# Sharing the first modulation between two engines, turning scaled rows, and moving modulation pieces between attentions

## The reference

```python
def adaln_modulation(c, w, b):
    mod = jax.nn.silu(c) @ w + b
    return [m[:, None, :] for m in jnp.split(mod, N_MOD, axis=-1)]
...
    for layer in range(DEPTH):
        shift_m, scale_m, gate_m, shift_f, scale_f, gate_f = adaln_modulation(c, *ada[layer])
        pre_m, post_m, pre_f, post_f = norms[layer]
        h = rmsnorm(x, pre_m) * (1.0 + scale_m) + shift_m
        x = x + gate_m * rmsnorm(mixers[layer](h), post_m)
        h = rmsnorm(x, pre_f) * (1.0 + scale_f) + shift_f
        x = x + gate_f * rmsnorm(swiglu(h, *ffns[layer]), post_f)
    return x
```

## Time and profile before

| | |
|---|---|
| median of three runs | 2046.96 us (2045.36 to 2047.48) |
| the profiled execution | 2044.72 us, span 2042.9 us |
| PE busy | 1922.0 us (94% of the span) |
| DVE busy | 1378.7 us (67%) |
| ACT busy | 986.7 us (48%) |
| POOL busy | 263.4 us (13%) |
| mean granted clock of PE | 0.978 |
| chain that ended last | PE 75%, DVE 14%, ACT 3%, issue 2% |

### The profile page before, as it was taken

One profiled execution on the slowest core, in us unless ns is written; L12 is line 12 of the kernel. 1 busy time (PEld: TensorE's weight loads), 2 busy tenths in 40 slices (PEclk: granted clock), 3 DMA queues, 4 the chain that ended last, 5 costly groups with the idle time before them and its releaser, 6 DMA issues.

```text
span 2042.9 us, 33499 instructions
## 1 busy us (share of the span) xinstructions
PE 1922.0 (94%) x13340; PEld 1773.0 (87%) x13340; DVE 1378.7 (67%) x2511; ACT 986.7 (48%) x1432; POOL 263.4 (13%) x121
## 2 busy tenths in 40 slices
PE   5899899988998789999998999999999999999998
PEld 5887799988967589998997889999998888999997
DVE  4898765647956664335756548988878887666665
ACT  5445544454435354445554545566653334444444
POOL 1001044430001024441000047100000000000000
PEclk8999999999999799999999999999999999999999
DMA  7663466645654245555444344477776866555452
GB/s 300 228 203 127 157 250 247 234 179 199 205 181 169 73 166 195 186 186 181 165 145 142 127 145 166 166 209 220 219 220 227 300 255 227 187 225 196 176 204 106
DMA packets 94234, 392.82 MB, mean 192 GB/s; under 512 B 7648, under 2 KB 41584, under 8 KB 55552
## 3 DMA queue, kind: packets, MB, share of 16 engines
q1 hardware_dynamic: 94080, 390.69, 55.0%
HBM read 372.83 MB, written 15.73 MB: 190 GB/s over the span
## 4 chain that ended last, share of the span: by engine, by line
PE 75%; DVE 14%; ACT 3%; issue 2%; DMA 0%; POOL 0%; DVEq 0%; ACTq 0%
PE ps L563 10%; PE ps L565 10%; PE ps L564 10%; PE acc L559 9%; PE acc L560 9%; PE acc L561 9%; DVE wlo L1281 3%; PE acc L563 3%; PE acc L565 3%; PE acc L564 3%; DVE arena L1310 2%; PE ps L1236 1%; PE acc L1236 1%; PE ps L626 1%; PE ps L1009 1%
## 5 line engine op out<-in xcount | busy, mean ns | idle before, releaser
L2300 ACT ACTIVATE whi<-raw 128x1024 fp32r<-128x1024 f32 x559 | 589.5, 1059 | 494.3 <-PE acc L561 274.1
L1281 DVE TENSOR_TENSOR wlo<-raw,whi 128x1024 fp32r<-128x1024 f32 x460 | 567.9, 1242 | 312.3 <-ACT whi L2300 311.4
L563 PE MATMUL ps<-hhi,whi 128*128 128x256 f32 x1824 | 521.2, 286 | 9.5 <-ACT hhi L2412 5.4
L564 PE MATMUL ps<-hlo,whi 128*128 128x256 f32 x1824 | 516.6, 283 | 0.0
L565 PE MATMUL ps<-hhi,wlo 128*128 128x256 f32 x1824 | 516.6, 283 | 0.0
L563 PEld LDWEIGHTS ps<-hhi,whi 128*128 128x128 f32 x1824 | 350.2, 192 | 14.6 <-ACT hhi L2412 6.1
L564 PEld LDWEIGHTS ps<-hlo,whi 128*128 128x128 f32 x1824 | 350.3, 192 | 2.9
L565 PEld LDWEIGHTS ps<-hhi,wlo 128*128 128x128 f32 x1824 | 350.1, 192 | 0.0
L1281 POOL TENSOR_TENSOR wlo<-raw,whi 128x1024 fp32r<-128x1024 f32 x99 | 245.2, 2480 | 683.1 <-ACT whi L2300 682.8
L559 PE MATMUL acc<-whi,chi 128*128 128x512 f32 x752 | 295.6, 393 | 3.5 <-DVE wlo L1281 1.9
L560 PE MATMUL acc<-whi,clo 128*128 128x512 f32 x752 | 294.0, 391 | 0.0
(11 more groups left out here) (443 smaller groups left out, 2418.6 us busy)
## 6 DMA issues: line engine op xcount, KB each, us to landing
raw<-in_peer_down SPq DMA_DIRECT2D x64, 1024.0 KB, 5.0
raw<-in_peer_up SPq DMA_DIRECT2D x64, 1024.0 KB, 5.1
arena<-in_ada SPq DMA_DIRECT2D x80, 512.0 KB, 4.8
raw<-in_w_gate SPq DMA_DIRECT2D x22, 1024.0 KB, 4.8
raw<-in_w_up SPq DMA_DIRECT2D x22, 1024.0 KB, 5.2
raw<-in_w_down SPq DMA_DIRECT2D x22, 1024.0 KB, 4.8
arena<-spill SPq DMA_DIRECT2D x14, 1024.0 KB, 7.0
spill<-hT_t SPq DMA_DIRECT2D x22, 448.0 KB, 6.4
```

The lines of the kernel that those rows point to most:

```text
L563: e.matmul(out, hi, xh, start=start, stop=False, skip_group_check=True)
L564: e.matmul(out, hi, xl, start=False, stop=False, skip_group_check=True)
L1281: e.tensor_tensor(out=lo, in0=w, in1=hi.bitcast(F32), op=ALU.subtract).then_inc(*X(("lo", j)))
L2300: e.activation(hi, w, ACT.Copy, scale=1.0).then_inc(*self.A(("hi", j)))
```

## The change

It has five parts.

1. The prologue's modulation: each of the four groups is shared. DVE does parts 0, 1, 4 and 5, ACT scales parts 2, 3, 6 and 7 (`BY_PE`), and PE sums those four and then DVE's sum. The first weight slab's transfer goes ahead of the last quarter's; piece 0's goes to just before slab 2. Three correction cuts leave POOL for DVE.
2. Norms: DVE scales the rows of x themselves (`ve_unit`), and PE turns them by transposes; `pe_rows` does transposes as well.
3. At the junctions, one cut of the next stage's first weights on ACT goes ahead between the squares, the one after it goes behind the high parts; DVE's goes behind the second tile (where the norm has shifts).
4. Seven modulation pieces leave the NSA stage (`ada=False`) and are done in GLA: two after w_ngate, three after the second compression, two ahead of the last head (`pe_pieces`, `ve_pieces`).
5. In NSA the normalisation of GLA's output moves ahead of w_nvs, cuts come ahead of the scores, and the turn of the compressed probabilities goes into the first branch.

```diff
-FIRST = (("w_low", 0, 0), ("w_low", 0, 1), ("w_low", 1, 0), ("w_glr", 0, 0), ("w_mqk", 0, 0))
+FIRST = (("w_glr", 0, 0), ("w_mqk", 0, 0))
+BY_PE = (2, 3, 6, 7)
...
     def pe_norm(...)
...
-            e.wait_ge(*self.at("diag", nm, tt))
             for j in range(8):
+                if j % 4 == 0:
+                    e.wait_ge(*self.at("unit", nm, tt, j // 4))
                 o = (j % 2) * 256 + tt * 128
-                i = e.matmul(self.banks.tile(nm, "turned", j // 2)[:, o:o + 128], x[:, tt, j * 128:(j + 1) * 128],
-                             m.diag[:, tt, :], start=True, stop=True, skip_group_check=True)
+                i = e.transpose(self.banks.tile(nm, "turned", j // 2)[:, o:o + 128], m.upd[:, tt, j * 128:(j + 1) * 128],
+                                m.ident)
...
     def pe_rows(...)
...
-                i = e.matmul(ps[:, j * 128:(j + 1) * 128], bc(col[:, 4 * half + j:4 * half + j + 1], [128, 128]), self.m.ident,
-                             start=True, stop=True, skip_group_check=True)
+                i = e.transpose(ps[:, j * 128:(j + 1) * 128], bc(col[:, 4 * half + j:4 * half + j + 1], [128, 128]),
+                                self.m.ident)
...
+    def pe_pieces(self, e, n):
+        for _ in range(n):
+            self.pe_ada(e)
...
     def pe_pro(...)
...
+            for k in BY_PE:
+                e.wait_ge(*self.at("scaled", g, k))
                 for j in range(4):
+                    e.matmul(ps[:, j * 128:(j + 1) * 128], m.ada4[:, g, k // 2, (k % 2) * 512 + j * 128:
+                                                                 (k % 2) * 512 + j * 128 + 128], m.ones,
+                             start=k == BY_PE[0] and j == 0, stop=False, skip_group_check=True)
+            e.wait_ge(*self.at("summed", g))
+            for j in range(4):
+                i = e.matmul(ps[:, j * 128:(j + 1) * 128], m.acc4[:, g, j * 128:(j + 1) * 128], m.ones, start=False,
+                             stop=True, skip_group_check=True)
...
     def pe_gla(...)
...
         t.then_inc(*self.P(("full", "w_ngate"), ("whole", "w_ngate", 0), ("gated", "P")))
+        self.pe_pieces(e, 2)
...
         self.pe_cmp_hidden(e, 1)
+        self.pe_pieces(e, 3)
         self.pe_cmp_turn(e, 1)
         e.wait_ge(*self.at("out", "gla_state", 2, 2))
         for h in range(4):
+            if h == 3:
+                self.pe_pieces(e, 2)
...
     def pe_nsa(...)
...
-        self.pe_linear(e, "w_nks", 0, 8, 2, m.hH, m.hL)
-        self.pe_linear_tok(e, "w_nvs", 0, 8, m.hH, m.hL)
+        self.pe_linear(e, "w_nks", 0, 8, 2, m.hH, m.hL, ada=False)
+        self.pe_linear_tok(e, "w_nvs", 0, 8, m.hH, m.hL, ada=False)
...
-                self.pe_out(e, "w_out1a", range(at, at + 2), m.cH, m.cL, at == 0, False, "mix1_post", "gla")
+                self.pe_out(e, "w_out1a", range(at, at + 2), m.cH, m.cL, at == 0, False, "mix1_post", "gla", ada=False)
...
-    def ve_diag(self, e, nm, tt):
+    def ve_unit(self, e, nm, tt, x):
         m = self.m
         e.wait_ge(*self.at("root", nm, tt))
-        e.tensor_scalar(out=m.diag[:, tt, :], in0=m.ident, scalar1=m.small[:, 50 + tt:51 + tt], scalar2=None,
-                        op0=ALU.mult).then_inc(*self.V(("diag", nm, tt)))
+        for half in range(2):
+            sl = slice(512 * half, 512 * half + 512)
+            e.tensor_scalar(out=m.upd[:, tt, sl], in0=x[:, tt, sl], scalar1=m.small[:, 50 + tt:51 + tt], scalar2=None,
+                            op0=ALU.mult).then_inc(*self.V(("unit", nm, tt, half)))
...
     def ve_gla(...)
...
         self.ve_windows(e, 0)
+        self.ve_pieces(e, 2)
...
         self.ve_windows(e, 1)
+        self.ve_pieces(e, 3)
         self.ve_cmp_turn(e, 1)
+        self.ve_pieces(e, 2)
...
     def se_junction(...)
...
         self.se_acc_square(e, post, 1, 0)
+        self.cut_hi(e, self.W.last(first, 0) + 1)
         self.se_x_square(e, norm, post, 0, 0)
...
     def se_normed(...)
...
-        if first:
-            self.cut_hi(e, self.W.last(first, 0) + 2)
         for jj in range(4):
...
+        if first:
+            self.cut_hi(e, self.W.last(first, 0) + 2)
...
     def sync(...)
...
         for g in range(4):
             for h in range(2):
+                if (g, h) == (3, 1):
+                    e.dma_start(self.W.slab(0)[0], D["w_low"][0]).then_inc(self.W.slots[0], 16)
...
-        self.sp_ada(e, 0)
...
+            if n == 0:
+                continue
+            if n == 2:
+                self.sp_ada(e, 0)
```

More of the change, by code:

```diff
@@ L736, in pe_pro @@
         m = self.m
-        self.pe_norm(e, "mix0", m.x)
+        self.pe_norm(e, "mix0")
         for g in range(4):
             ps = self.banks.take(e, "mod", g)
[L740 to L748, removed]
-                for j in range(4):
-                    i = e.matmul(ps[:, j * 128:(j + 1) * 128], m.acc4[:, g, j * 128:(j + 1) * 128], m.ones, start=j == 0,
-                                 stop=True, skip_group_check=True)
+            for k in BY_PE:
+                e.wait_ge(*self.at("scaled", g, k))
+                for j in range(4):
+                    e.matmul(ps[:, j * 128:(j + 1) * 128], m.ada4[:, g, k // 2, (k % 2) * 512 + j * 128:
[5 more added lines that the diff above has]
+                             stop=True, skip_group_check=True)
             i.then_inc(*self.P(("full", "mod", g)))
@@ L922, in pe_mix1 @@
         self.P.mark("end", "ffn0", "P")
-        self.pe_norm(e, "mix1", m.x)
+        self.pe_norm(e, "mix1")
         self.banks.order = ALL
@@ L1084, in pe_mix2 @@
         self.P.mark("end", "ffn1", "P")
-        self.pe_norm(e, "mix2", m.x)
+        self.pe_norm(e, "mix2")
         self.banks.order = ALL
@@ L1178, in pe_route @@
         m = self.m
-        self.pe_norm(e, "peer", m.x)
+        self.pe_norm(e, "peer")
         self.banks.order = ALL
@@ L1311, in ve_ada, with ve_pieces @@
                                            op1=ALU.add).then_inc(*V(*([("ada", s)] if k else [])))
+    def ve_pieces(self, e, n):
+        for _ in range(n):
+            self.ve_ada(e)
     def ve_ada_until(self, e, layer, part):
@@ L1384, in ve_normed @@
         whole(1)
+        if first:
+            self.cut_lo(e, V, self.W.last(first, 0) + 1)
         low(0)
@@ L1453, in ve_sum @@
         self.ve_eps(e, norm, 0, 48)
-        self.ve_diag(e, norm, 0)
+        self.ve_unit(e, norm, 0, self.m.x)
         self.ve_add_x(e, post, 1, 1)
@@ L1874, in ve_nsa @@
                     *V(*([("hvx",)] if ht and j == 3 else [])))
-        self.ve_linear(e, "w_nks", 0, 8, 2)
-        self.ve_linear_tok(e, "w_nvs", 0, 8)
-        e.wait_ge(*self.at("full", "vb"))
-        e.tensor_tensor(out=m.vb, in0=bc(self.banks.tile("vb")[:, 0:64].unsqueeze(1), [128, 8, 64]),
-                        in1=bc(m.kc("ind").unsqueeze(2), [128, 8, 64]), op=ALU.mult).then_inc(*V(("out", "vb")))
+        self.ve_linear(e, "w_nks", 0, 8, 2, ada=False)
         e.wait_ge(*self.at("rstd", "gla"))
@@ L1888, in ve_nsa @@
                 *V(("normed", "gla", j)))
+        self.ve_linear_tok(e, "w_nvs", 0, 8, ada=False)
+        e.wait_ge(*self.at("full", "vb"))
+        e.tensor_tensor(out=m.vb, in0=bc(self.banks.tile("vb")[:, 0:64].unsqueeze(1), [128, 8, 64]),
+                        in1=bc(m.kc("ind").unsqueeze(2), [128, 8, 64]), op=ALU.mult).then_inc(*V(("out", "vb")))
         for eng in "PA":
@@ L1925, in ve_nsa @@
                 self.ve_scores(e, f"nsa{qt}{br}", 8, nk, 0.125, lambda hs, n: m.ab[:, qt, hs, 0:nk], m.St1,
-                               gate=m.ng[:, qt, 8 + 8 * br:16 + 8 * br])
-                self.ve_out(e, "w_out1a", range(at, at + 2))
+                               gate=m.ng[:, qt, 8 + 8 * br:16 + 8 * br],
+                               ahead=self.W.last("w_out1a", 2 * at + 1, 512) + 2)
+                self.ve_out_by_rows(e, "w_out1a", range(at, at + 2), ada=False)
                 self.ve_turn(e, f"nsa{qt}{br}", 8, nk, m.PT1[br])
-            e.wait_ge(*self.at("full", "pct", qt))
-            e.tensor_copy(m.pct, self.banks.tile("pct", qt)[:, 0:128]).then_inc(*V(("out", "pct", qt)))
+                if br == 0:
+                    e.wait_ge(*self.at("full", "pct", qt))
+                    e.tensor_copy(m.pct, self.banks.tile("pct", qt)[:, 0:128]).then_inc(*V(("out", "pct", qt)))
             self.ve_bank_split(e, f"nsa{qt}", m.hH, m.hL, qt)
@@ L2378, in se_junction, with se_norm @@
         self.se_root(e, norm, 1, 48)
-    def se_norm(self, e, nm, src, at=48, ahead=None):
+    def se_norm(self, e, nm, src, at=48, ahead=None, first=None):
         for tt in range(2):
             for half in range(2):
+                if tt and half and first:
+                    self.cut_hi(e, self.W.last(first, 0) + 1)
                 self.se_x_square(e, nm, src, tt, half, at)
@@ L2694, in se_nsa @@
                 at = 4 * qt + 2 * br
+                self.cut_hi(e, self.W.last("w_out1a", 2 * at + 1, 512) + 2)
                 self.se_scores(e, f"nsa{qt}{br}", 8, nk, m.St1)
```

(2 more changed lines are left out.)

105 lines of the change are left out of this document (60 added, 45 removed).

## The result

The changed kernel takes 2032.26 us (median of four runs, 2030.82 to 2034.59) against 2046.16 for the kernel before (four runs). The ratio is 0.9931, with a 95% interval of 0.9916 to 0.9947: faster by 14 us, between 11 and 17. I had said 2025 within 2010 to 2042, so the time is 7 us above the forecast and a third of the gain did not come. The profiled execution took 2031.83 us with a span of 2030.0; it is 12.9 us shorter in span than the profiled execution before, and that difference can be followed place by place, since both kernels do the same 10,920 matmuls of their products in the same order. A trace is one execution, though: where two kernels have the same code, their traces can still differ by some us (the experiments show by how much).

What follows compares the result with a forecast made beforehand. PE (TensorE) carries the chain nearly everywhere, so only its waits, low clock and shortenable work can pay. -5 - 11 - 4.5 - 6.9 + 6 = -21.4 on 2044.72: 2023, or 2025 by medians; 8 in 10: 2010 to 2042.

Steps and rivals of the forecast that it cites:

- The prologue (-5): Modulation sums before the first projections: PE's sums end sooner, first projection matmul near 40 to 41 instead of 45.67; -5 us.
- Rows by transposes, norms, junctions (-11.4): Gate and final rows -4.5 us; norms as scaled rows turned by transposes, at five junctions and two other norms, -6.9.
- the clock (+6): At five junctions the shorter norms leave the projection's first matmuls at 1.2 GHz; +6 us, bounds 0 and 13.
- rival B: Transposes keep PE's clock low, so 28 projection matmuls after each of five junctions run slow: 13 instead of 6, 2032; chance 0.25.
- The pieces (-11): Modulation pieces moved from sparse to linear attention: sparse attention gains 11.2 to 12.2 us besides a first part; net -11.
- the stall in linear attention: PE waits about 4 us for a piece ahead of head 3, plus two sums of 0.9 each: 5 to 6 us.
- the first part: Start of the compressed scores in sparse attention: DVE ready about 6 us sooner without two pieces ahead of it.
- the order of sparse attention: Moved normalisation and cuts change DVE's order, not its amount of work: nothing, bounds -2 and +2 us.
- A: No stall in linear attention, since the pieces arrive in time: 6 us better, 2019; chance 0.13.
- C: Linear attention takes back all that sparse attention gives, its stall longer or at two places: +11, 2036; chance 0.12.
- D: Slower: the lower clock after transposes lasts so long that it eats all gains, 27.4 us without the clock; chance 0.05.
- E: Within 0.2% (4 us): transposes cost as much as two-record matmuls, arrival bounds the prologue, pieces' time only moves; chance 0.05.

Runs made afterwards that it cites:

- the variant with transposes alone: The changed kernel with each of the norms' transposes done twice, 32 records of transposes; span 2035.4 us against the change's 2030.0, one run.
- the matmul variant: The changed kernel with the norms' 16 transposes replaced by matmuls by the identity, 32 records; span 2034.0 us against the change's 2030.0, one run.

## Why the prediction was right or wrong

**The prologue (-5): right.** PE's sums ended at 36.23, at the good end of the 36.1 to 38.8 that I had worked out, since the clock stayed up; the lead at w_xbc's second slab was 5.03, and alone the part gave 5.5 by time.

**Rows by transposes, norms, junctions (-11.4) and the clock (+6): right in sum, a little too good.** Outside the prologue and the two attentions the lead grew by 4.1 us where I had 5.4; it is the difference of two traces, and stages with the same code differ by as much from trace to trace. By place, from the last product ahead to the first projection matmul, the norms gave 0.6 us at ffn0, 1.5 at mix1, 0.2 at ffn1, 1.9 at mix2 and -1.0 at peer, 3.2 of the 4.7 that I had; the memory and cross-attention norms gave 1.4 and 1.2, where I had 0.5 and 1.75. The three gate rows outside sparse attention gave 0.95 each. The gate rows are 32 records of 4.3 us now, against 64 of 8.1:

```profile
L639 PE MATMUL ps<-kc_t,gs_t 128*128 128x128 f32 x32 | 4.3, 277 | 2.9 <-DVE gs_t L1424 2.9
```

The wait ahead of them rose from 1.8 to 2.9 us, as allowed for. The clock's charge was right in size: the lead falls behind the first projection matmul by 1.44 us at ffn0, 0.4 at mix1, 1.46 at ffn1, 0.8 at mix2 and 1.67 at peer, 5.8 together. With it the five junctions are 2.6 us longer than before: what the transposes save there, the clock takes back and more. But the charge's ground was half right. I had the projection starting inside one low stretch; in the profiled execution there are two of 3.4 us at ffn0 with full clock between them, and the second follows PE's stand behind the transposes. Peer, which I had at 0, lost 1.0 us, through the cut between its squares: with that cut behind the last root its first matmul comes 0.1 us sooner than in the kernel before.

**Transposes and the clock (rival B): refuted, though the time came out at its figure.** The time is 2032, the very number of rival B, for another reason. The Trainium skill (TensorE: Matmul & The Clock Gate, Part 4: PE-mode transpose) says that full clock doesn't engage for transposes. In the variant with transposes alone, which run from 237.68 to 243.76, the granted clock rose from 0.50 to 1.00 at 242.6. The measurement decides: here they lift the clock, as far as the matmul variant's do.

**The pieces (-11): the step that failed.** I wrote that the stall in linear attention "eats the first part's gain (worth 6) and leaves the 11". The two attentions together gave 3.8 us (lead 6.61 to 10.42). In the forecast's own terms, the first part, up to w_out1a, gave the 6 (5.9), the stretch behind it 6.3 of the 11, and linear attention took back 8.3 where I had 5 to 6. Three things were wrong. First, the 11. The waits for the heads fell as I said, and the first half's heads took 4.0 us instead of 7.2. But PE then stood at the transposes instead, 3.3 us and 3.7 us (waits above), and the low clock moved along with the waits: the products of the first half's second branch ran at 1.2 GHz,

```profile
652.50:659.30 6.80, 6.80 (x25) 5.51 (x24) 5.87 (x18) 3.63 (x17) 0.00 (x0) 0.50 0.45 155
```

and took 8.1 us where they had taken 5.7. In the three traces of the same code with less of the low clock, this stretch gave 9.4 to 10.3, near the 11; in the profiled execution the clock took 4 of it. Second, the order of sparse attention, which I priced at nothing within 2: by the ratios it is worth 6.8, and the 6 of the first part come only with it. Third, linear attention. The wait itself was as forecast, 4.71 against "about 4", with the cause that I had named, the transfer behind w_out1a's slabs; the two sums at 0.9 each were as forecast too. What I left out was the clock behind the wait, 1 us on the sum and 1 on head 3. And nothing absorbed it: with the sum later, w_nks starts 6.8 us sooner, and the ratio is better by 7 us. The time lies inside the range of 8 in 10, but just above the forecast's own of 2018 to 2032: the other terms were near, and this one missed by 7 us.

**The rivals.** A fell: the wait is there. C was near in its effect, though not by its mechanism (the stall was of the forecast length, and at one place): linear attention took back more than the pieces gave (8.3 against 4.9 to 6.0), and in the variant with the order as before the two attentions together lose 2.1 us. D and E did not come about.

## What to carry to other kernels

When work is moved to where an engine is idle, check the instruction of the bottleneck engine that waits for its result: here DVE had half of 23 us free, but PE's sum stood ahead of a head that needed nothing from it, and moving that one sum behind the next 5.7 us of ready work was worth about 7 us. A wait on PE costs more than its length, since the clock falls in it and the next work pays; price a stall with the records behind it at 1.2 GHz. And an edit that "only" changes the order on an engine with a chain of waits is not worth nothing: it has to be followed through the chain like any other; here the order and the moved pieces gave 0.9 and 1.2 us alone ahead of w_out1a and 5.9 together. Last, one trace of a long stretch is one draw: before a difference in it is put down to an edit, look at other traces with the same code there.

## What the hardware showed that I had not expected

Transposes alone brought the granted clock from 0.50 to 1.00 (at 242.6 us, while they ran). A stand of PE as short as 2.1 us behind 3.3 us of work was followed by a second fall in the profiled execution, so that in place of one low stretch of 6.8 us there were two of 3.4 with 3.4 us at full clock, half of it idle, between them; other executions of the same junction had one of 10.2. And the same stretch of sparse attention, with PE's longer waits alike (3.3 to 3.4, 3.7 and 1.9 us), took 81.8 us in one execution and 85.8 in another, with 10.2 and 20.5 us at the lower clock in it.
